# Broadcasts by transpose, column sums between weight tiles, and a gather by row tile in a float32 two-model kernel

## The reference, cut to what matters

```python
def layer_norm(x, g, b):
    mu = mean(x); var = mean(square(x - mu))
    return (x - mu) * rsqrt(var + LN_EPS) * g + b
def rmsnorm(x, w):
    return x * rsqrt(mean(x * x) + EPS) * w
# end of the first block
x = layer_norm(DEEPNORM_ALPHA * x + y, ln_g, ln_b)
# second block
for layer in range(2):
    hn = rmsnorm(x, norm1_w[layer]) * (1 + scale1) + shift1
    y = mlstm_mixer(hn, ...) if layer == 0 else hgrn2_mixer(hn, ...)
    x = x + gate1 * y
    hn = rmsnorm(x, norm2_w[layer]) * (1 + scale2) + shift2
    y = swiglu(hn, ...) if layer == 0 else moe_swiglu(hn, ...)
    x = x + gate2 * y
return rmsnorm(x, final_norm_w)
```

## Time and profile before

| | us |
|---|---|
| median of 3 runs (lowest, highest) | 2013.81 (2013.07, 2014.88) |
| profiled execution, its own time | 2011.94 |
| its span, first to last instruction | 2009.9 |
| TensorE busy in the span | 1966.3 (98%) |
| VectorE / GpSimd / ACT busy | 863.7 / 677.5 / 568.1 |
| mean granted TensorE clock | 0.991 of full |

### The profile page before, as it was taken

How to read it: one execution, slowest core, us unless ns; L and a number is a source line. 1 busy time by engine, 2 the same in 40 slices (tenths; PEclk the granted TensorE clock), 3 DMA queues, 4 the chain that set the end, 5 groups by cost and what they waited for, 6 DMA issues and landing times. The chain is left out here.

```text
span 2009.9 us, 28716 instructions
## 1 busy us (share of the span) xinstructions
PE 1966.3 (98%) x11096; PEld 1665.5 (83%) x11096; DVE 863.7 (43%) x1177; ACT 568.1 (28%) x1210; POOL 677.5 (34%) x582
## 2 busy tenths in 40 slices
PE   8999998999999999999999999999999999999997
PEld 7778644888647888888869999755999999999996
DVE  3898586666425444455246667633100000000023
ACT  1443113555413111110045566522110210111101
POOL 5666331655314444444436666511200000000011
PEclk9999997999999999999999999999999999999999
DMA  8214730222124666621221111102957568678884
GB/s 332 76 53 176 276 137 23 100 84 77 66 73 169 210 207 210 205 89 60 98 84 64 43 64 64 53 11 75 310 192 241 193 228 275 242 243 311 326 326 158
DMA packets 82712, 312.68 MB, mean 156 GB/s; under 512 B 10137, under 2 KB 10657, under 8 KB 82449
## 3 DMA queue, kind: packets, MB, share of 16 engines
q1 hardware_dynamic: 75952, 289.73, 41.0%
q0 software_dynamic: 4320, 13.76, 2.0%
q10 hardware_dynamic: 2304, 7.33, 1.0%
HBM read 301.43 MB, written 9.36 MB: 155 GB/s over the span
## 5 line engine op out<-in xcount | busy, mean ns | idle before, releaser
L3087 PE MATMUL banks<-sb_act,sb_ring 128*128 128x192 f32 (+3 forms) x3696 | 500.9, 298 | 2.1 <-DMA sb_ring<-in_w_moe_up 1.3
L3087 PEld LDWEIGHTS banks<-sb_act,sb_ring 128*128 128x128 f32 x3696 | 498.3, 191 | 3.2 <-DMA sb_ring<-in_w_moe_up 1.8
L287 PE MATMUL banks<-sb_x_norm,sb_ring 128*128 128x256 f32 x1224 | 288.5, 380 | 2.1 <-ACT sb_ring L451 2.1
L287 PEld LDWEIGHTS banks<-sb_x_norm,sb_ring 128*128 128x128 f32 x1224 | 230.2, 190 | 37.0 <-issue 6.2
L3413 DVE TENSOR_TENSOR sb_act<-sb_work,banks 128x128 f32<-128x128 f32 (+3 forms) x88 | 27.7, 315 | 505.2 <-PE banks L3087 498.1
L426 POOL TENSOR_TENSOR sb_ring<-sb_ring 128x512 f32<-128x512 f32 x146 | 207.1, 1418 | 105.9 <-PE banks L287 46.8
L2954 POOL DMA_INDIRECT sb_work<-first_expert_rows,sb_table x8 | 7.5, 937 | 461.3 <-DMA first_expert_rows<-sb_x_norm 459.1
L287 PE MATMUL banks<-sb_work,sb_ring 128*128 128x256 f32 x640 | 150.6, 380 | 1.0 <-ACT sb_ring L451 1.0
L287 PEld LDWEIGHTS banks<-sb_work,sb_ring 128*128 128x128 f32 x640 | 120.2, 190 | 16.8 <-issue 1.2
L3213 ACT ACTIVATE sb_work<-banks 128x128 f32<-128x128 f32 (+3 forms) x88 | 26.3, 298 | 309.9 <-PE banks L3087 304.9
L1511 PE MATMUL banks<-sb_act,sb_ring 128*128 128x512 f32 x256 | 112.4, 594 | 0.0
(11 more groups left out here) (518 smaller groups left out, 3023.9 us busy)
## 6 DMA issues: line engine op xcount, KB each, us to landing
sb_ring<-in_w_moe_up SPq DMA_DIRECT2D x176, 512.0 KB, 4.7
sb_ring<-in_w_moe_down SPq DMA_DIRECT2D x64, 704.0 KB, 5.6
sb_act<-in_cond_w SPq DMA_DIRECT2D x84, 512.0 KB, 3.5
sb_ring<-in_w_ffn_up SPq DMA_DIRECT2D x44, 512.0 KB, 4.3
sb_ring<-in_w_h_in SPq DMA_DIRECT2D x32, 512.0 KB, 4.1
sb_ring<-in_w_in SPq DMA_DIRECT2D x28, 512.0 KB, 6.3
sb_ring<-in_w_m_in SPq DMA_DIRECT2D x24, 512.0 KB, 4.6
sb_ring<-in_w_ffn_down SPq DMA_DIRECT2D x16, 704.0 KB, 5.3
```

What stands on the lines that cost most here:

```text
L287: last = m.nc.tensor.matmul(out, lhs(k), rhs(k), start=(k == 0 and not onto), stop=(k == n - 1), skip_group_check=onto)
L3087: last = nc.tensor.matmul(ps[:, b % BANKS, 0:cap], w, act, start=(k == 0), stop=(k == kt - 1))
```

## The change

The names of the change cover six edits:

1. Both kinds of `spread` (L631, L1346) use `tensor.transpose` of the broadcast column in place of a matmul with the identity.
2. The 20 column sums are put between the last output tile's matmuls, 4 after each of the last five.
3. On VectorE two products for the second variance are put behind the inverse root of the first.
4. A head's norm matmul (L534) is put behind the next head's scores, for heads 0 to 5.
5. In `stage_m` GpSimd's first differences wait until VectorE has scaled 5 of the 8 tiles.
6. The gather runs for its first two output tiles row tile by row tile, into banks 6 and 7, each step waiting only for its own row tile; the expert's first block waits for the evacuated inputs one by one.

```diff
@@ TokenNorm.spread
-            last = m.nc.tensor.matmul(m.ps[:, 7, rows(t, P)], self.inv[:, t:t + 1].broadcast_to([P, P]), m.c("ident"),
-                                      start=True, stop=True)
+            last = m.nc.tensor.transpose(m.ps[:, 7, rows(t, P)], self.inv[:, t:t + 1].broadcast_to([P, P]),
+                                         m.c("ident"))
@@ stage_out, tensor
-            piece(KD - 1, 3, 8)
-            pe.wait_ge(centred, 3)
-            pe.wait_ge(added, KD - 1)
+            piece(KD - 1, 3, 5)
             for c, acc in enumerate((x_sum, xg_sum, xgb_sum, sq_sum, gsq_sum)):
+                piece(KD - 1, 5 + c, 6 + c)
+                if c == 0:
+                    pe.wait_ge(centred, 3)
+                if c == 3:
+                    pe.wait_ge(added, KD - 1)
                 for t in range(ST):
                     nc.tensor.matmul(stat_col(t, c), acc[:, rows(t, P)], m.ones1024[:, 0:1], start=(c == 0 and t == 0),
                                      stop=False)
-            piece(KD - 1, 8, 10)
...
-                    last = nc.tensor.matmul(ps[:, bank, rows(t, P)], values[:, t:t + 1].broadcast_to([P, P]),
-                                            m.c("ident"), start=True, stop=True)
+                    last = nc.tensor.transpose(ps[:, bank, rows(t, P)], values[:, t:t + 1].broadcast_to([P, P]),
+                                               m.c("ident"))
@@ stage_out, vector
-            step(nc.vector.tensor_tensor(first, first, xxg, ALU.add))
-            step(nc.vector.scalar_tensor_tensor(cross, x0, mean_gb, xgb, ALU.mult, ALU.add))
             dve.wait_ge(rooted, 1)
             step(nc.vector.reciprocal(inv, root))
             give(dve, nc.vector.tensor_tensor(shifted, x0, inv, ALU.mult), inverse, 1)
+            step(nc.vector.tensor_tensor(first, first, xxg, ALU.add))
+            step(nc.vector.scalar_tensor_tensor(cross, x0, mean_gb, xgb, ALU.mult, ALU.add))
@@ stage_m, tensor
                 last.then_inc(score, 1)
+                if h >= 2:
+                    norms[h - 2].pe(m, pe)
...
-                if h:
-                    norms[h - 1].pe(m, pe)
+            norms[HEADS - 2].pe(m, pe)
             totals(HEADS - 1)
@@ stage_m, gpsimd
+            pool.wait_ge(m.rms_half, norm_in.scaled + KD - 3)
             for which in (T1, T3, T2, T4):
                 pairs.combine(pool, 0, which)
@@ stage_moe
-    x0_banks = (0, 1, 2, 3, 6, 7)
+    x0_banks = (6, 7, 0, 1, 2, 3)
+    x0_first = 2
...
-            pe.wait_ge(first_slots, 1)
-            pe.wait_ge(row_out, ST)
-            for k in range(KD):
...
+            for t in range(ST):
+                pe.wait_ge(first_slots, t + 1)
+                pe.wait_ge(row_out, t + 1)
+                for k in range(x0_first):
+                    gather_first(k, t)
+            for k in range(x0_first, KD):
                 if k >= len(x0_banks):
                     pe.wait_ge(x0_out, k - len(x0_banks) + 1)
                 for t in range(ST):
...
+                    gather_first(k, t)
...
-                    if first_pass(p) and r == 0:
-                        pe.wait_ge(x0_out, KD)
-                    else:
+                    if not (first_pass(p) and r == 0):
                         pe.wait_ge(turned_out, p * GATHERS + (need[r] - 1))
...
                         for k in range(kt):
+                            if first_pass(p) and r == 0 and b == 0:
+                                pe.wait_ge(x0_out, max(x0_first, k) + 1)
@@ stage_moe, vector
-                if t < ST - 1:
-                    step(last)
-            give(dve, last, first_slots, 1)
+                give(dve, last, first_slots, t + 1)
```

8 lines of the change are left out of this document (5 added, 3 removed).

## The result

| | before | changed |
|---|---|---|
| median, timed side by side (lowest, highest; 4 runs each) | 2013.44 us (2012.13, 2014.88) | 1997.03 us (1995.59, 1998.49) |
| ratio, 95% interval | | 0.9915 (0.9902 to 0.9929) |
| a second timing, later (9 and 5 runs) | 2012.73 us (2009.93, 2015.77) | 1997.97 us (1996.33, 2000.17) |
| ratio, 95% interval | | 0.9932 (0.9919 to 0.9946) |
| profiled execution, its span | 2009.9 us | 1994.0 us |

The change gains 16.4 us in the first timing and 14.8 in the second; 13.8 were forecast. The sign and most of the mechanisms held. What was missed is a matter of one or two us in each of a few places, and it takes executions side by side to see which of them belong to the change.

The account below looks back on a forecast made before the run. TensorE, busy 98% of the span, was taken as the bound. Terms 4.2 + 2.3 + 0.2 + 1.9 + 0.9 + 4.3 = 13.8 us, from the 2013.81 us median, gave 2000.0 us; range 1997 to 2005.

Parts of the forecast that it names:

- The one fall that did get a term, in the gather: Ahead of the first expert: the clock stays up because the idle gap shrinks from 1.94 to 0.4 us; 1.7 us.
- GpSimd's 2.6: Tile loop: what holding GpSimd back could give beyond its 0.2 us if no VectorE add met GpSimd (upper bound 2.8).
- Divided sums: End of the first block: column sums between wide matmuls keep the clock up and cover a wait; 4.2 us (0.7 to 5.0).
- The rival in which the clock falls among the divided sums: First block's end: clock falls at 304.0 all the same, gain there 0.7 instead of 4.2 us; 2003.5 us, chance 0.18.
- To the next stage: From the copy of the sums to the next stage's first tile: halved broadcasts and moved products gain 2.3 us.
- GpSimd's hold: Tile loop: GpSimd's later start moves the stall from tiles 2 to 4 to tiles 6 to 8; 0.2 us (-1.7 to +2.8).
- Later broadcasts: Two broadcasts right ahead of stage barriers: transposes halve TensorE's 0.94 us each; 0.9 us together (0 to 0.9).
- Heads: Norm matmuls behind the next scores no longer wait 0.73 and 1.19 us for ACT's square; 1.9 us (0 to 1.9).
- Gather: Ahead of the first expert: earlier start 1.6, last wait 0.85, clock staying up 1.7; 4.3 us in all.
- the case without this gain: Gather ahead of the first expert: if the clock falls again, the gain is 2.6 us instead of 4.3.
- The rival on transposes: Transposes do not keep the clock up: falls at two later stage ends, 1.7 us each; 2003.4 us, chance 0.12.
- the prediction's rival on the low clock: Tile loop and next block stay at 1.2 GHz, VectorE's pace hiding the first 11 us; 2015.7 us, chance 0.03.

Follow-up runs that it names:

- the three with filled gaps: Changed kernel with three output-product matmul groups moved into the last heads' two waits: 1993.19 and 1995.28 us; with the last expert's gathers also spread, 1992.19 us.

## Why the prediction was nearly right and where it failed

**The step that failed.** The fall of the clock at the last head got no term. The profile of before had it, and the prediction, which added up terms of edits alone, carried it into the changed kernel without a word; in the profile after it was absent, and that gave 1.69 us (L1631 4.08, L1633 2.39). The one fall that did get a term, in the gather, was charged to the wait ahead of it. Both were read from a single execution as if they belonged to the kernel. The range had the same fault: its lower end was built from what the edits might give beyond the sum, 1.0 us for sums and broadcasts and some of GpSimd's 2.6, and left out that the clock can be lost and kept at places that no edit touches. Each such fall is 1.5 to 1.7 us in dense work, and the rows of one execution can't say whether it is there each time. With one of them to either side the range would have reached to 1995.

**Divided sums.** The mechanism, the start of L1339 (306.73, forecast 306.8) and the waits it removes were right. For the last sums the forecast took half of what the clock can give (half of 3.5 - 1.84 is 0.83, it wrote 0.9); from L1337 to the copy it went from 4.05 to 2.42 us, 1.63. In two of the thirteen executions with divided sums the fall came inside the last ones (1.85 and 1.44 us for L1342), in the other eleven at their end or behind them (1.03 to 1.06). That makes the pair of profiles' 4.96. But the 4.2 of the forecast is no worse a number than that, because the old order varies: from the start of L696 to the copy it took 19.79, 19.58, 19.01 and 18.26 us in the four executions with the sums in a row, by where the clock fell, and 14.80 to 14.83 in eleven of the thirteen with divided sums (15.21 and 15.63 in the other two). By these means the edit is worth 4.3 us, by execution 2.6 to 5.0. The rival in which the clock falls among the divided sums was not seen in any execution with them.

**To the next stage.** 2.27 us for a forecast of 2.3, and its parts 1.81 (transposes) and 0.46 (products) as worked out. **GpSimd's hold** 0.56 for 0.2: that the stall moves and doesn't go was right, and the first meeting, which is only a part of an add, was left out. **Later broadcasts** 0.89 for 0.9.

**Heads.** 2.46 for 1.9. The idle times that stand in the rows were added up, and they are smaller than what the reordering gives, by 0.27 us in each place. The starts of the records show where that lies. In the profile of before the record ahead of L534 starts 1.01 us sooner than L534 at 411.49, where L534 waits, and 0.11 sooner at 504.55, where it doesn't: the wait costs 0.90, and 0.73 is listed as idle. And from L534 to the next matmul it is 1.06 us behind the wait and 0.95 without it. So 0.17 + 0.11 us come on top of 0.73; at 459.36 they are 0.16 + 0.11 on top of 1.19.

```profile
504.55 1.02 PE L534 MATMUL banks<-sb_work,sb_ones 128*128 128x512 f32 x2
```

**Gather.** 4.3 forecast, 4.31 in the pair of profiles, and that is luck. The term held 1.7 us for a fall of the clock inside the gather as if the gap of 1.94 us caused it (and its three parts, 1.6, 0.85 and 1.7, add up to 4.15); with a gap of 1.94 the fall was there in one execution of two, with one of 1.3 to 1.4 in none of three. Whether the shorter gap of 0.28 us keeps it away is not shown, since it was mostly absent without it. At equal clock the edit is worth 2.5 to 2.8 us, which is the 2.6 that the forecast gave for the case without this gain.

**How the pair adds up.** By themselves the edits give 4.96 + 2.27 + 0.55 + 2.46 + 0.89 + 2.63 = 13.76 us in this pair of profiles, and with the mean of the sums 13.1. The pair adds 1.69 at the last head and 1.68 in the gather, and loses 1.22 to the waits in the last expert and the end: 15.91. So the edits came out at the 13.8 of the forecast, but by two errors that cancel, 1.7 us too much for the gather and 1.7 too little in sums, heads and hold. The second timing's gain is 14.8 us, that of the first 16.4. The kernel before gave 2010.2 to 2013.4 us in the five timings, in two of them by a single run, so a gain of this size is not known to better than some 1.5 us from one timing.

**The rival on transposes** was half right. With transposes the clock was low until 319 to 323 us (327 in the kernel with the sums in a row), in the tile loop; in the five executions with matmul broadcasts it rose within about half a us of the broadcasts' end, in the changed kernel with that part undone at 316.4, though in four of the five it fell again for some three us a little later, in the tile loop. Whether that is the kind of instruction or only its shorter time isn't told apart. But the loop runs at VectorE's pace, and its last wait was 0.26 us, so the longer low stretch cost nothing, as the prediction's rival on the low clock had it (the first 11 us hidden). The two later stage ends showed no fall in any of the seventeen. The Trainium skill, "TensorE: Matmul & The Clock Gate", Part 4 (PE-mode transpose), says that the full clock does not engage for transposes. In the kernel before it did, in a run of nothing else:

```profile
1392.00:1392.50 0.50, 0.50 (x5) 0.50 (x4) 0.43 (x3) 0.44 (x1) 0.00 (x0) 0.50 0.00 0
1392.50:1393.00 0.50, 0.50 (x4) 0.50 (x3) 0.43 (x3) 0.50 (x1) 0.00 (x0) 0.58 0.00 0
1393.00:1393.50 0.50, 0.50 (x6) 0.29 (x4) 0.43 (x3) 0.17 (x1) 0.00 (x0) 1.00 0.00 0
```

TensorE ran L2999 alone from 1390.08 to 1393.4. In all seventeen profiles the clock was low as the turned rows began or fell within 0.1 us of it. In ten it was back after some three us, in the first batch of transposes or just at its end, in two after some seven us, and in five after some ten, within half a us of the end of the second batch and ahead of the gather. So the rule as it stands isn't borne out, and what decides between three us and ten isn't settled here.

## What to carry to other kernels

Thin matmuls in a long run cost twice here, by themselves and by the clock that the wide ones behind them lose: put them between wide ones, and leave a group for the place where TensorE would wait. A wait of TensorE is worth more than the idle time listed for it (0.27 us more at each of two waits): take it from the starts of the records. Where only a broadcast of a column is wanted in float32, a transpose of the broadcast column does it in half the records. And before a term is built on a fall of the clock, look for it in a second execution: one that comes and goes belongs in the range and not in the sum.

## What was not expected of the hardware

That the falls come and go. In seventeen profiles one came with the run of 20 sums each time the run was there (inside it in 3, 0.7 us behind it in 1), and with divided sums one in or behind the last sums each time (13). But the fall at the last head was there in 3, one inside the old gather in 1 of 5, one at 1275 us, behind a wait of 1.5 us, in 3, and one among the last expert's waits in 3 of the 8 that had the early waits (1927 to 1942 us). The waits ahead were there without a fall in the others: at the last head in 11 (the three with filled gaps have none), at 1275 us in 14, with the same 1.5 us.

In the last expert the DMA engines were busy all the time for a while: over 1910 to 1930 us of the changed kernel they moved 411 GB/s at a share of 1.02 to 1.03, and the rows gathered by GpSimd (q0) took 42.2% of it beside 53.4% for the weights (q1).

```profile
DMA packets 2244, 8.23 MB, mean 411 GB/s; under 512 B 239, under 2 KB 239, under 8 KB 2243
...
q1 hardware_dynamic: 1179, 4.31, 53.4%
q0 software_dynamic: 920, 3.38, 42.2%
```
